# Pool mixer: weight and row factor in one VectorE step, products scaled by ScalarE, last squares summed by matmuls

## What is computed

```python
x = rmsnorm(h, norm_final)               # end of the first block
h = rmsnorm(x, mix_norm[0])
# per group g of 256 channels, window w = (2, 4, 8, 16)[g]:
y_g = trailing_mean(h_g, w) - h_g
x_g = x_g + (y_g @ pool_w[g] + pool_b_g) * pool_scale_g
x = x + conv_ffn_2(rmsnorm(x, ffn_norm[0]), ...)    # F2 below
```

## Time and profile before

| | us |
|---|---|
| median of three runs (1162.0 to 1164.17) | 1162.36 |
| the profiled execution | 1162.03 |
| its span | 1160.2 |
| TensorE busy | 1121.6 |
| VectorE busy | 797.1 |
| ScalarE busy | 594.8 |
| GpSimd busy | 4.7 |

### The profile page before, as it was taken

The page is one execution under the profiler, slowest core; times in us unless marked ns, Lnnn a source line. Parts: engine busy times, 40 slices in busy tenths (PEclk is TensorE's granted clock), DMA queues, the critical chain, the costliest instruction groups (busy, mean ns, idle before and its releaser), DMA issues.

```text
span 1160.2 us, 21441 instructions
## 1 busy us (share of the span) xinstructions
PE 1121.6 (97%) x9266; PEld 1095.0 (94%) x9266; DVE 797.1 (69%) x1180; ACT 594.8 (51%) x809; POOL 4.7 (0%) x10
## 2 busy tenths in 40 slices
PE   4999999999999999999999899999999989999998
PEld 4898999999998799999999899999999879999998
DVE  5876578776557777877657697774558756977741
ACT  5465456454347665554445365454447644654530
POOL 0000000000000000000001000000000000000000
PEclk9999999999999999999999899999999999999999
DMA  7443246555445045655553175555555423755540
GB/s 293 166 149 119 97 151 218 177 180 197 164 148 197 20 169 186 218 172 183 198 179 143 41 250 182 182 170 205 191 171 169 132 110 111 253 181 182 168 175 21
DMA packets 30238, 191.98 MB, mean 165 GB/s; under 512 B 4289, under 2 KB 5441, under 8 KB 9921
## 3 DMA queue, kind: packets, MB, share of 16 engines
q1 hardware_dynamic: 30144, 190.62, 47.8%
HBM read 189.56 MB, written 1.05 MB: 164 GB/s over the span
## 4 chain that ended last, share of the span: by engine, by line
PE 91%; DVE 5%; ACT 2%; issue 1%; DMA 1%; SPq 0%; ACTq 0%; DVEq 0%
PE bank L336 29%; PE bank L337 28%; PE bank L338 28%; DVE wlo L1294 2%; PE TB L455 1%; ACT whi L893 1%; PE bank L475 1%; DMA raw<-in_a_qkv 1%; PE SB L781 1%; PE SB L787 1%; PE SB L440 1%; PE SB L442 1%; PE SB L370 1%; PE bank L479 1%; PE bank L557 1%
## 5 line engine op out<-in xcount | busy, mean ns | idle before, releaser
L1294 DVE TENSOR_TENSOR wlo<-raw,whi 128x2048 fp32r<-128x2048 f32 (+2 forms) x183 | 402.4, 2202 | 107.8 <-ACT whi L893 107.8
L336 PE MATMUL bank<-xx,whi 128*128 128x256 f32 x1408 | 400.2, 284 | 6.0 <-DVE xx L1299 6.0
L338 PE MATMUL bank<-xx,wlo 128*128 128x256 f32 x1408 | 399.4, 284 | 0.0
L337 PE MATMUL bank<-xx,whi 128*128 128x256 f32 x1408 | 399.4, 284 | 0.0
L893 ACT ACTIVATE whi<-raw 128x2048 fp32r<-128x2048 f32 (+2 forms) x183 | 335.8, 1839 | 100.5 <-PE bank L338 94.3
L336 PEld LDWEIGHTS bank<-xx,whi 128*128 128x128 f32 x1408 | 271.3, 193 | 6.2 <-issue 6.2
L337 PEld LDWEIGHTS bank<-xx,whi 128*128 128x128 f32 x1408 | 271.3, 193 | 0.0
L338 PEld LDWEIGHTS bank<-xx,wlo 128*128 128x128 f32 x1408 | 271.2, 193 | 0.0
L336 PE MATMUL bank<-hx,whi 128*128 128x256 f32 x704 | 199.2, 283 | 0.0
L337 PE MATMUL bank<-hx,whi 128*128 128x256 f32 x704 | 199.2, 283 | 0.0
L338 PE MATMUL bank<-hx,wlo 128*128 128x256 f32 x704 | 199.2, 283 | 0.0
(11 more groups left out here) (149 smaller groups left out, 1247.7 us busy)
## 6 DMA issues: line engine op xcount, KB each, us to landing
raw<-in_gate SPq DMA_DIRECT2D x44, 1024.0 KB, 4.9
raw<-in_up SPq DMA_DIRECT2D x44, 1024.0 KB, 4.9
raw<-in_down SPq DMA_DIRECT2D x32, 1024.0 KB, 4.9
raw<-in_a_qkv SPq DMA_DIRECT2D x12, 1024.0 KB, 5.9
raw<-in_down SPq DMA_DIRECT2D x16, 768.0 KB, 4.3
raw<-in_d_qkv SPq DMA_DIRECT2D x12, 1024.0 KB, 4.9
raw<-in_a_o SPq DMA_DIRECT2D x4, 1024.0 KB, 4.9
raw<-in_b_o SPq DMA_DIRECT2D x4, 1024.0 KB, 5.1
```

What stands on the lines that cost most here:

```text
L336: e.matmul(po, ah, bh, start=start, stop=False, skip_group_check=True)
L337: e.matmul(po, ah, bl, start=False, stop=False, skip_group_check=True)
L338: return e.matmul(po, al, bh, start=False, stop=stop, skip_group_check=True)
L1294: e.tensor_tensor(wlo[n % RING][:, 0:nk * w], raw[n % RAW][:, 0:nk * w], whi[n % RING][:, 0:nk * w].bitcast(F32), ALU.subtract).then_inc(s ...
```

## The change

The sums stand ahead of the linear map on TensorE. The squares of the last pair of tiles are neither scaled on ScalarE nor added on VectorE: four matmuls multiply `sq` by a two-column operand, `gain2`, with a one in the first column and `norm_final` squared in the second, and add to the same PSUM columns. VectorE multiplies `xT` by `norm_final` and by `rb` in one step of eight instructions. GpSimd's steps are gone. ScalarE writes the window products, scaled and with the scaled bias, to a new tile `pu`; VectorE adds `pu` to `xT`, one instruction of 128x512 for a group. `lo(u + 4)` and `hi(u + 5)` stand behind F2's inputs. `n_add` only counts the additions, of which the pool mixer now has two.

```diff
@@ -204,6 +205,7 @@
         ident = cst("ident")
         rcol, rv, rt = small[:, 0, 0:2], small[:, 1, 0:2], small[:, 2, 0:2]
         gg, bs = small[:, 7, 0:8], small[:, 8, 0:8]
+        gain2 = small[:, 9, 0:4].rearrange("p (m w) -> p m w", m=2)
         tcol, lv, ly, lt = small[:, 12, 0:4], small[:, 13, 0:4], small[:, 14, 0:4], small[:, 15, 0:4]
         va, ra, ta = small[:, 4, 0:4], small[:, 5, 0:4], small[:, 6, 0:4]
         mask0 = cst("mask0").unsqueeze(1).to_broadcast([128, 2, 384])
...
@@ -253,6 +255,10 @@
         def n_res(s, c):
 
             return 4 * s + c + 1
+
+        def n_add(s, c):
+
+            return 3 * s + c - (s > POOL)
 
         LAYER = {F0: 0, F1: 1, F2: 2, F3: 3}
         MIX = {A: 0, B: 1, DD: 2}
...
@@ -835,13 +841,30 @@
                 s = POOL
                 u = first[s]
                 wh, wl = unit(u)
-                weights_here(u)
-                for g in range(NG):
+
+                def both_sums():
+
+                    e.wait_ge(s_ones, 1)
+                    e.wait_ge(s_add, n_add(s, 2))
+                    e.wait_ge(s_add2, 2)
+                    for h in range(2):
+                        for w, src in ((0, ssum), (1, ssum2)):
+                            for c in range(2):
+                                e.matmul(SB[:, 0, 2 * h + w:2 * h + w + 1], src[:, c, h * 128:(h + 1) * 128],
+                                         ones[:, 0:1], start=(h == 0 and w == 0 and c == 0), stop=False,
+                                         skip_group_check=True)
+                    e.wait_ge(s_gg, 1)
+                    e.wait_ge(s_sq, n_res(s - 1, 3) + 4)
+                    for h in range(2):
+                        for c in range(2):
+                            last = e.matmul(SB[:, 0, 2 * h:2 * h + 2], sq[:, c, h * 128:(h + 1) * 128],
+                                            gain2[:, c, :], start=False, stop=(c == 1), skip_group_check=True)
+                    last.then_inc(s_sum, 1)
+
+                def linear(g):
                     b = bk(s, g)
-                    if g == 2:
-                        norm_sums(s)
-                        e.wait_ge(s_add2, 3)
-                        token_sums(ssum2, SB[:, 1, :]).then_inc(s_sum2, 1)
+                    if g == 0:
+                        weights_here(u)
                     for k in (2 * g, 2 * g + 1):
                         x_here(s, k)
                         for h in range(2):
@@ -849,6 +872,10 @@
                             last = three(b[:, h * 256:(h + 1) * 256], xx[:, k, 0, sl], xx[:, k, 1, sl], wh[:, k, :],
                                          wl[:, k, :], k == 2 * g and h == 0, k == 2 * g + 1)
                     last.then_inc(s_used if g == 3 else s_pp, 1)
+
+                both_sums()
+                for g in range(NG):
+                    linear(g)
                 row(s, 0)
                 e.wait_ge(s_win, 16)
                 for g in range(NG):
...
@@ -901,8 +928,10 @@
                         e.wait_ge(s_sum, s)
                     e.activation(ssum[:, :, :], xT[:, 0:2, :], ACT.Square).then_inc(s_sq, 1)
                     return
-                if s or c > 1:
-                    e.wait_ge(s_add, 3 * s + c - 1)
+                if c > 1:
+                    e.wait_ge(s_add, n_add(s, c - 1))
+                elif s:
+                    e.wait_ge(s_add, n_add(s - 1, 3 if s - 1 != POOL else 2))
                 e.activation(sq[:, :, :], xT[:, 2 * c:2 * c + 2, :], ACT.Square).then_inc(s_sq, 1)
 
             def scaled_squares(c):
@@ -918,7 +947,7 @@
 
                 e.wait_ge(s_res, n_res(s - 1, c))
                 squares(s, c)
-                if s == POOL:
+                if s == POOL and c < 3:
                     scaled_squares(c)
                 split_x(s, 2 * c)
                 split_x(s, 2 * c + 1)
...
@@ -1243,9 +1272,17 @@
                         last = e.activation(zz[:, h, g * 256:(g + 1) * 256], b[:, h * 256:(h + 1) * 256], ACT.Copy,
                                             scale=ra[:, 2 + h:3 + h])
                     last.then_inc(s_zz, 1)
+                for g in range(NG):
+                    b = bk(s, g)
+                    e.wait_ge(s_zw, g + 1)
+                    for m, k in ((0, 2 * g), (1, 2 * g + 1)):
+                        last = e.activation(pu[:, k, :], b[:, m * 256:(m + 1) * 256], ACT.Identity,
+                                            scale=vcol("pool_scale", k), bias=bs[:, k:k + 1])
+                    last.then_inc(s_uu, 1)
+                    if g:
+                        next_input(F2, g - 1)
+                next_input(F2, 3)
                 hi(u + 5)
-                for g in range(NG):
-                    next_input(F2, g)
 
             e.wait_ge(s_vec, 16)
...
@@ -1354,9 +1391,9 @@
                 e.tensor_tensor(xp, bk(s, c if s in MIX else 2 + c)[:, :], xp, ALU.add).then_inc(s_res, 1)
 
             def next_input(s, c):
-                if c:
+                if c and (s, c) != (POOL, 3):
                     add_squares(s, c)
-                if s == POOL and c:
+                if s == POOL and c in (1, 2):
                     add_scaled(c)
                 split_x(s, 2 * c)
                 split_x(s, 2 * c + 1)
...
@@ -1690,16 +1727,19 @@
             def pool_gains():
                 v = lambda name: vec[:, VEC_AT[name]:VEC_AT[name] + 8]
                 e.tensor_tensor(gg, v("norm_final"), v("mix_norm_2"), ALU.mult)
-                e.tensor_tensor(bs, v("pool_b"), v("pool_scale"), ALU.mult).then_inc(s_gg, 1)
+                e.tensor_tensor(bs, v("pool_b"), v("pool_scale"), ALU.mult)
+                e.memset(gain2[:, :, 0:1], 1.0)
+                last2 = vec[:, VEC_AT["norm_final"] + 6:VEC_AT["norm_final"] + 8].unsqueeze(2)
+                e.tensor_tensor(gain2[:, :, 1:2], last2, last2, ALU.mult).then_inc(s_gg, 1)
                 e.wait_ge(s_gg, 1)
 
             def pool_mixer():
                 s = POOL
                 u = first[s]
                 e.wait_ge(s_sum, s + 1)
-                e.tensor_scalar(va[:, 0:2], SB[:, 0, 0:2], 1.0 / D, EPS, ALU.mult, ALU.add)
-                e.wait_ge(s_sum2, 1)
-                kept(e.tensor_scalar(va[:, 2:4], SB[:, 1, 0:2], 1.0 / D, None, ALU.mult))
+                sums = SB[:, 0, 0:4].rearrange("p (h w) -> p h w", h=2)
+                e.tensor_scalar(va[:, 0:2], sums[:, :, 0], 1.0 / D, EPS, ALU.mult, ALU.add)
+                kept(e.tensor_scalar(va[:, 2:4], sums[:, :, 1], 1.0 / D, None, ALU.mult))
                 after_own()
                 kept(e.scalar_tensor_tensor(out=va[:, 2:4], in0=va[:, 0:2], scalar=EPS, in1=va[:, 2:4], op0=ALU.mult,
                                             op1=ALU.add))
@@ -1707,28 +1747,20 @@
                 norm_diag(s, ra)
                 norm_row(s, 0)
                 e.wait_ge(s_rb, ROW[s])
-                for g in range(2):
-                    kept(e.tensor_tensor(xT[:, 2 * g:2 * g + 2, :], xT[:, 2 * g:2 * g + 2, :], rbb, ALU.mult))
-                after_own()
+                e.wait_ge(s_xh, n_x(s, KD - 1))
                 for k in range(KD):
-                    if k >= 4 and k % 2 == 0:
-                        e.wait_ge(s_x0p, k // 2 - 1)
-                    last = e.tensor_scalar(xT[:, k, :], xT[:, k, :], vcol("norm_final", k), bs[:, k:k + 1], ALU.mult,
-                                           ALU.add)
-                kept(last)
-                after_own()
-                lo(u + 4)
+                    kept(e.scalar_tensor_tensor(out=xT[:, k, :], in0=xT[:, k, :], scalar=vcol("norm_final", k),
+                                                in1=rb[:, :], op0=ALU.mult, op1=ALU.mult))
                 for g in range(NG):
-                    b = bk(s, g)
-                    e.wait_ge(s_zw, g + 1)
-                    for m, k in ((0, 2 * g), (1, 2 * g + 1)):
-                        last = e.scalar_tensor_tensor(out=xT[:, k, :], in0=b[:, m * 256:(m + 1) * 256],
-                                                      scalar=vcol("pool_scale", k), in1=xT[:, k, :], op0=ALU.mult,
-                                                      op1=ALU.add)
-                    last.then_inc(s_res, 1)
+                    xp = xT[:, 2 * g:2 * g + 2, :]
+                    e.wait_ge(s_uu, g + 1)
+                    if g == 0:
+                        after_own()
+                    e.tensor_tensor(xp, xp, pu[:, 2 * g:2 * g + 2, :], ALU.add).then_inc(s_res, 1)
                     if g:
                         next_input(F2, g - 1)
                 next_input(F2, 3)
+                lo(u + 4)
 
             e.memset(ones[:, :], 1.0).then_inc(s_ones, 1)
             for k in range(4):
...
@@ -1756,9 +1788,6 @@
 
 
         def gpsimd_program(e):
-            e.wait_ge(s_rb, ROW[POOL])
-            for g in range(2, NG):
-                e.tensor_tensor(xT[:, 2 * g:2 * g + 2, :], xT[:, 2 * g:2 * g + 2, :], rbb, ALU.mult).then_inc(s_x0p, 1)
             e.wait_ge(s_used, first[DD])
             for b in bm:
```

(7 more changed lines are left out.)

## The result

The changed kernel takes 1156.03 us in the median of four runs (1155.35 to 1158.35) against 1162.49 for the kernel before: a ratio of 0.9947, 95% interval 0.9934 to 0.996. It is faster, by 6.5 us; 6.98 were forecast. The profiled execution took 1155.42 (before 1162.03), its span is 1153.5 (before 1160.2).

The account below looks back on a forecast made before the run. TensorE, 97% busy, bounds the kernel; time can fall where it stands still or runs slowly, chiefly around its 6.0 us wait before F2. F2's start 4.64 earlier plus clock 2.34 gives 6.98 us: 1155.4, range 1154.0 to 1157.8.

Parts of the forecast that it names:

- row matmuls later: Pool mixer, TensorE: with all sums ahead of the linear products, row matmuls start at 631.8 instead of 631.41, cost 0.39 us.
- two passes to one: Pool mixer, VectorE: eight fused steps take 3.28 us, ending at 636.29; 5.95 us passed before; gain 2.67 us.
- weight split moved: VectorE ahead of F2: lo(u+4) moves behind F2's inputs and leaves the path, gain 2.29 us.
- first pair of F2: F2's first 96 matmuls on TensorE take 11.52 us instead of 13.86 if the clock stays up, gain 2.34 us.
- the interference: VectorE's passes lost 1.92 us beside GpSimd's steps; were that worth nothing, 0.75 us of the 2.67 would be left.
- The cover of lo(u+4): The moved split would run from about 645.6 to 648, before F2's first sums at 650.3; priced at nothing.
- The inputs of F2: F2's start: tile 2's low part ready at 641.3, wanted at 641.6; margin 0.3 us, no cost.
- The clock: Before F2: fell after 3.03 us idle of 3.40, stayed with 2.33 of 4.00; 1.1 us idle is well under both.
- The one that the clock falls: Rival, 14%: clock still falls after the shorter gap or in the small matmuls, taking back its gain: 1157.7 us.
- The slower case: Rival, 3%: half clock from the pool mixer's head through products and windows, 2.0 us slower, 1164.4; needs about 14 us.
- ScalarE was not late: Rival, 10%: ScalarE's activations of group 2 or 3 push F2's tile 2 or 4 past its need, half a microsecond, 1155.9.
- nothing was absorbed behind F2: Rival, 3%: the gain is absorbed by a later wait of F2 or the attention behind it on weights, 1162.4 us.

Follow-up runs that it names:

- the two experiments: The kernel before with only lo(u+4) moved behind F2's last input: 1159.89 us; the changed kernel with lo(u+4) put back between fused steps and additions: 1159.14 us.
- the trace with GpSimd beside: Changed kernel plus two unused 128x512 GpSimd multiplications beside the fused steps; one run, 1160.8 us (time not used), the eight steps 5.41 us instead of 3.25.
- three traces of other versions: Changed kernel with sums behind linear products of groups 0 and 1 (median 1157.27), with unused GpSimd multiplications (1160.8), or with window products taken by VectorE (median 1158.55).

## Why the prediction was right

Step by step, in the changed kernel's profiled execution, with F1's 0.12 us taken off:

| step | forecast | measured |
|---|---|---|
| row matmuls later | 0.39 | 0.51 (631.92 for 631.41) |
| copy of the row | as before | gain 0.11 (1.10 for 1.21 to the first step) |
| two passes to one | gain 2.67 | gain 2.59 (3.36 for 5.95) |
| weight split moved | gain 2.29 | gain 2.29 in the chain; 2.19 and 2.01 in the two experiments |
| addition of products | gain 0.07 | gain 0.09 (0.76 for 0.85) |
| F2's start | 4.64 earlier | 4.57 earlier |
| TensorE idle | 1.1 | 1.04 |
| first pair of F2 | gain 2.34 | gain 2.11 |
| sum, F2's start and first pair | 6.98 | 6.68 |

The mechanism is the one forecast, step for step. That the median of four came within 0.6 us of the forecast 1155.4 is in part luck: falls of the clock that the sum doesn't hold spread single runs from 1153.93 to 1161.48. The median of all fifteen, 1155.57, is nearer.

- **The sums on TensorE.** The eight records of the two-column matmuls took 0.89 us, not the 0.79 of the one-column ones, and make most of the 0.12 us by which the row came later than forecast. That it would wait for the products and not for the diagonal held: the diagonal was done at 629.57.
- **The fused steps** took 3.25 us for 3.28. Of the alternatives weighed there, the interference was real: 2.16 us in the experiment for 1.92 read from the earlier trace rows. My sentence that 0.75 us would be left without it mixed two things, though; without GpSimd and unfused, VectorE needs 5.24 us, so fusing alone is worth 1.9 against VectorE doing both passes by itself.
- **The cover of lo(u+4)** held: it ran from 645.27 to 647.56, and F2's sums came at 650.5. The next load was issued 6.7 us later (647.58 for 640.89) and nobody waited. hi(u+5) ran from 644.54 to 646.44 and was in nobody's way; it was moved in no experiment by itself.
- **The inputs of F2.** Tile 2's low part was done at 641.3, as forecast, and TensorE asked for it at 641.9, so the margin was 0.6 us and not 0.3. ScalarE's pairs of products took 1.0, near the upper bound of 1.10 that I took.
- **The clock** is the term that was mis-sized, by 0.23 us: 96 matmuls at full clock take 11.75 us to the first sum in the chain, and I had 11.52 from 0.12 each, which leaves out the longer first matmul and the drain before the sums. The reading of when it falls stood on few rows. It named 3.03 us idle of 3.40 as a case of a fall, and the experiment with the split put back, with 3.04 idle, agrees. It named the stretch from 104.50 to 108.50, with 2.33 idle of 4.00, as one where the clock stays; but in the trace with GpSimd beside, the clock fell in just that stage, at about 107.2, at waits of 1.44 and 0.91 us, as long as those in the kernel before (1.42 and 0.91). So 1.1 us of idle time was less safe than the prediction said, though before F2 the clock held in every trace with a gap of 1.04 or 1.22 us. And the clock's 2.1 us are not a gain beside the others; they come because all the others together shorten the gap.
- **The rivals.** The one that the clock falls, in the small matmuls too, had 14%. It did not happen in the profiled execution, but the fall in the small matmuls did in three traces of other versions, two of them with the same head of the mixer; it costs 1.5 or 3.0 us in those two. TensorE stood still nowhere ahead of that fall. The slower case needed half clock for 14 us; the longest fall seen in the pool mixer was 6.9. ScalarE was not late, and nothing was absorbed behind F2. The gain column took two small VectorE steps, not three, in front of F1 (439.9).

## What to carry to other kernels

Where the busiest engine stands still, look first for work on the late engine that merely stands there in program order: one weight split moved behind the inputs was worth 2.0 to 2.3 us of 6.7 at no cost. An engine called in to help can slow the one that it helps; take its help away in an experiment before adding more. A gap of TensorE has a second price, the clock after it, which falls away only once the gap is short enough, so several small cuts can be worth more together than their sum. And a mean clock tells that a run was slowed, not where: look at the stretches of more than one trace before blaming a stage.

## What the runs showed of the hardware

- GpSimd's two 128x512 multiplications (2.71 us) made eight `scalar_tensor_tensor` steps of VectorE take 5.41 us instead of 3.25; single steps grew from 0.47 to as much as 1.60.
- The granted clock fell to half ahead of F2 behind gaps of TensorE of 3.04, 3.20, 3.81, 5.30 and 6.01 us, and not behind 1.04 (four traces) and 1.22.
- Near 30 us, where every version has the same kind of gap, its length differs from execution to execution: the clock held behind 2.28, 2.30 and 2.41 us, and fell behind the eleven others, 2.45 to 3.26. In the attention mixers it fell in four traces behind gaps of 0.9 to 1.9 us with short work between them (half clock from about 107.2 in one, from about 921.7, 927 and 930 in the others), and held in the other ten at like gaps.
- It also fell where TensorE never stood still, in or right behind 2.6 us of matmuls with one and two columns, in three of the nine traces of versions that keep the 24 records in one piece.
